# Projection weight loads moved from SyncE to ScalarE, and two weight splits moved by one slot, in a two-layer decoder step

## What is computed

```python
def fox_project(h, w_qkvf, b_f):
    q, k, v, f = jnp.split(h @ w_qkvf, [D_MODEL, 2 * D_MODEL, 3 * D_MODEL], axis=-1)
    logf = jax.nn.log_sigmoid((f + b_f).astype(jnp.float32))
def fox_attend(q, cum_q, q_pos, k, v, cum_kT, k_pos):
    s = jnp.einsum('bqhd,bkhd->bhqk', q, k) * (HEAD_DIM ** -0.5)
    s = s + jnp.transpose(cum_q, (0, 2, 1))[..., None] - cum_kT[:, :, None, :]
    p = jax.nn.softmax(jnp.where(mask, s, NEG_INF), axis=-1)
    return jnp.einsum('bhqk,bkhd->bqhd', p, v)
```

## The kernel before

| step | tile 3i+4 | tile 3i+5 | tile 3i+6 |
|---|---|---|---|
| load, SyncE | slot 0 (from pair 1 on), line 658 | slot 4, line 654 | slot 8, line 656 |
| high half, ScalarE | slot 2, line 1347 | slot 6, line 1377 | slot 12, line 1422 |
| low half, GpSimd | round 3, line 917 | round 7, line 919 | round 14, line 924 |

## Time and profile before

### The profile page before, as it was taken

One profiled execution on the slowest core, in us unless ns is written; L12 is line 12 of the kernel. 1 busy time (PEld: TensorE's weight loads), 2 busy tenths in 40 slices (PEclk: granted clock), 3 DMA queues, 4 the chain that ended last, 5 costly groups with the idle time before them and its releaser, 6 DMA issues.

```text
span 2634.0 us, 45278 instructions
## 1 busy us (share of the span) xinstructions
PE 2559.6 (97%) x18462; PEld 2344.4 (89%) x18462; DVE 1657.1 (63%) x1948; ACT 966.3 (37%) x1838; POOL 1532.8 (58%) x870
## 2 busy tenths in 40 slices
PE   7899999999899999999999999999999999999999
PEld 5677666666589999999999999999989999999998
DVE  5677666676556566666666663444466666666665
ACT  4466766667745322222222241111432222222223
POOL 2867566686237866666666652222586666666661
PEclk9999999999999999999999999999999999999999
DMA  8777777877731111111211111111111121111112
GB/s 292 248 254 250 265 267 272 294 251 257 260 105 50 57 49 49 49 49 53 61 49 49 57 33 49 48 45 32 53 49 49 51 61 51 49 49 49 49 57 82
DMA packets 240573, 292.33 MB, mean 111 GB/s; under 512 B 12995, under 2 KB 193316, under 8 KB 240246
## 3 DMA queue, kind: packets, MB, share of 16 engines
q1 hardware_dynamic: 216658, 271.40, 31.8%
q10 hardware_dynamic: 23572, 17.12, 2.0%
q0 software_dynamic: 144, 1.05, 0.1%
HBM read 268.28 MB, written 21.28 MB: 110 GB/s over the span
## 4 chain that ended last, share of the span: by engine, by line
PE 78%; POOL 8%; DVE 5%; issue 3%; ACT 2%; DMA 2%; SPq 0%; DVEq 0%; POOLq 0%; ACTq 0%
PE PS L2079 32%; PE PS L1634 10%; PE PS L2171 6%; PE PS L2172 6%; PE PS L2170 6%; PE PS L2007 6%; POOL kpage L867 4%; PE PS L1850 2%; DMA kpage<-in_cache_k 2%; PE PS L1852 2%; PE PS L1851 2%; PE PS L1790 1%; DVE pt L2428 1%; DVE s_raw L2365 1%; PE PS L2043 1%
## 5 line engine op out<-in xcount | busy, mean ns | idle before, releaser
L840 POOL TENSOR_TENSOR w_lo<-raw,w_hi 128x1024 fp32r<-128x1024 f32 (+2 forms) x98 | 245.1, 2501 | 641.2 <-ACT w_hi L1539 282.8
L2079 PE MATMUL PS<-a_all,wb 128*128 128x258 f32 x3488 | 571.5, 284 | 5.2 <-POOL wb L1000 3.6
L2079 PEld LDWEIGHTS PS<-a_all,wb 128*128 128x128 f32 x3488 | 486.5, 190 | 6.1 <-POOL wb L1000 4.0
L2687 DVE TENSOR_TENSOR x_res<-PS,x_res 128x1032 f32<-128x1032 f32 (+2 forms) x400 | 399.5, 1015 | 75.0 <-PE PS L2172 65.2
L867 POOL TENSOR_TENSOR kpage<-kpage,q_bc 128x1024 f32<-128x1024 f32 x128 | 307.3, 2416 | 102.1 <-DMA kpage<-in_cache_k 79.2
L2079 PE MATMUL PS<-c_lo,wb 128*128 128x258 f32 x1744 | 352.5, 284 | 0.0
L2171 PE MATMUL PS<-wb,w_hi 128*128 128x344 f32 x960 | 308.0, 321 | 0.0
L2172 PE MATMUL PS<-wb,w_lo 128*128 128x344 f32 x960 | 307.8, 321 | 0.0
L2170 PE MATMUL PS<-wb,w_hi 128*128 128x344 f32 x960 | 305.7, 318 | 0.0
L2079 PEld LDWEIGHTS PS<-c_lo,wb 128*128 128x128 f32 x1744 | 271.8, 190 | 0.0
L1634 PE MATMUL PS<-a_all,w_hi 128*128 128x344 f32 x1152 | 213.4, 321 | 0.4 <-ACT rinv L1129 0.4
(11 more groups left out here) (351 smaller groups left out, 5467.1 us busy)
## 6 DMA issues: line engine op xcount, KB each, us to landing
kpage<-in_cache_k SPq DMA_DIRECT2D x128, 512.0 KB, 4.7
vpage<-in_cache_v SPq DMA_DIRECT2D x128, 512.0 KB, 5.3
raw<-in_w_ffn_in SPq DMA_DIRECT2D x88, 512.0 KB, 4.2
raw<-in_w_ffn_out SPq DMA_DIRECT2D x44, 512.0 KB, 3.6
raw<-in_attn_w_qkvf SPq DMA_DIRECT2D x24, 512.0 KB, 6.1
vpage<-in_attn_w_qkvf SPq DMA_DIRECT2D x24, 512.0 KB, 6.1
raw<-in_conv_w_in SPq DMA_DIRECT2D x24, 512.0 KB, 3.7
out<-raw ACTq DMA_DIRECT2D x16, 512.0 KB, 7.0
```

The source lines that it names most:

```text
L840: gp.tensor_tensor(w_lo[s][:, 0:kts, 0:cols], raw[s][:, 0:kts, 0:cols], w_hi[s][:, 0:kts, 0:cols].bitcast(F32), ALU.subtract).then_inc(w_l ...
L2079: ins = pe.matmul(out[:, b, :], w[:, k, :], h[:, k, x, b * (HN // 2):(b + 1) * (HN // 2)], start=k == 0 and n == 0, stop=k == HK - 1 and n ...
L2687: ins = dve.tensor_tensor(x[:, at:at + n, :], src, x[:, at:at + n, :], ALU.add)
```

## The change

The three `load_q` calls go from SyncE's pair loop to ScalarE's, where a function of the same name issues the same transfers with the same wait. They come after `key_rows` in slot 0, after `total` in slot 5 and after the exponentials of slot 10. On ScalarE the high half of tile 3i+4 goes from slot 2 to slot 3, behind the exponentials, and that of tile 3i+5 from slot 6 to the end of slot 7. On GpSimd the low half of tile 3i+5 goes from round 7 to round 8; the other two low halves and the high half of tile 3i+6 stay where they are. The five loads issued ahead of the pair loop stay on SyncE.

```diff
@@ SyncE, pair(i) @@
             for n in range(NSLOT):
-                    if n == 4 and i < LAST:
-                        load_q(3 * i + 5)
-                    if n == 8 and i < LAST - 1:
-                        load_q(3 * i + 6)
-                    if n == 0 and 0 < i < LAST:
-                        load_q(3 * i + 4)
@@ GpSimd, pair(i) @@
                     if n == 3 and i < LAST:
                         low_q(3 * i + 4)
-                    if n == 7 and i < LAST:
+                    if n == 8 and i < LAST:
                         low_q(3 * i + 5)
@@ ScalarE @@
+            def load_q(n):
+
+                act.wait_ge(w_lod[w_slot(n - 1)], w_count(n - 1))
+                act.dma_start(raw[0][:, :, :], w_tile(w_qkvf, 0, KT, n % 3 * D + n // 3 * P)).then_inc(w_raw[0], 16)
@@ ScalarE, pair(i) @@
                 key_rows(i)
+                if 0 < i < LAST:
+                    load_q(3 * i + 4)
                 sample(0)
...
                 normalise(i, 7)
-                if more:
-                    high_q(3 * i + 4)
                 sample(2)
 
                 exponentials(i, 3)
                 if not more:
                     high_values(i)
+                if more:
+                    high_q(3 * i + 4)
                 total(i, 6)
...
                 total(i, 5)
+                if more:
+                    load_q(3 * i + 5)
                 sample(5)
...
                 sample(6)
-                if more:
-                    high_q(3 * i + 5)
-                else:
+                if not more:
                     early_tile(0)
 
                 exponentials(i, 7)
                 high_turned(i, 2)
                 total(i, 4)
+                if more:
+                    high_q(3 * i + 5)
                 sample(7)
...
                 exponentials(i, 10)
+                if i < LAST - 1:
+                    load_q(3 * i + 6)
                 store_output(i, 3)
```

## The result

The kernel after takes 2645.5 us (median of 6 runs, 2643.2 to 2646.9), the kernel before 2634.1 us (median of 6, 2631.9 to 2637.2). The ratio is 1.004, with an interval of 1.003 to 1.005: **11.4 us slower**. The forecast was 2636 us in a range from 2622 to 2648; the time lies in the range and outside the 0.2% that the text counted as no change. It is closest to rival 1, 2643 us. The forecast's own change, +3.2 us, was 8.2 us short.

The account below looks back on a forecast made before the run. TensorE's matmuls were taken to bound the pair loop, with 20.6 us open. Terms -3.5 + 8.7 - 4 + 2 = +3.2 us on the 2632.4 us median gave 2636 us, range 2622 to 2648.

Parts of the forecast that it names:

- rival 1: Slower: GpSimd's lateness at the key split is paid in full, gains of the later value split are lost; 2643 us, chance 0.25.
- Part A: Weight loads leave SyncE's page queue for ScalarE's: 19 of 24 move, no page was held back by them; 0 us.
- Part B: Value weights' high split goes from slot 6 to 7 on ScalarE, so slot 7's exponentials start earlier; -3.5 us.
- The first paragraph: Pair loop's first seven pairs: TensorE's matmuls cover 555.3 of 575.9 us, so at most 20.6 us can be won.
- Part C: Key weights' low split on GpSimd in slot 3 starts later, so pages behind it reach VectorE late; +8.7 us.
- Part D: Value weights' low split on GpSimd goes behind slot 8's pages, ending VectorE's waits for them; -4 us.
- Part E: Same load bytes at other times, slots 5 and 10, beside key pages whose landings may lengthen; +2 us.
- Rival 3: Slower: slot 5's load lands too late for slot 7's split, stopping ScalarE in all seven pairs; 2649 us, chance 0.05.
- Rival 2: Faster: the late key split is caught up, the value split's gains come in full; 2619 to 2623 us, chance 0.25.

## Why the prediction was right and wrong

- **Part A, 0 us: right.** The two runs that differ in the issuing queue lie 0.9 us apart, inside their intervals. By the Trainium skill's DMA: Bandwidth & Descriptors, section Issuing engines are not separate DMA queues, a new issuer could save the issues' time; these runs agree that it gives no more, and show not even that.
- **Part B, -3.5 us: wrong, it is about 0.** The step that failed is the subtraction "without the split the exponentials could start 0.95 us earlier". They did. But the step went from there straight to the end time, without asking whether TensorE waited for them. In slots 7 and 8 of the kernel before it stood still in two pairs: 0.96 us in pair 4, for another piece of ScalarE's work, and 0.51 us in pair 5, for these exponentials:

```profile
549.57 0.50 PE L1790 MATMUL PS<-k_hi,q_hi 64*128 64x512 f32 x2 [0.51 <-ACT probs L1192]
```

Slot 7 of pair 5 takes 4.7 us in all six kernels with the split in slot 7, and 5.3 us in the other eight. But slot 8 of that pair takes 5.8 to 6.1 us in the six and 5.4 in the others: what one slot won the next gave back. The first paragraph had the number to ask with, 20.6 us open, and never cut it by slot: 8.3 us are in slots 0 and 1, 8.6 in slots 11 to 14, 3.7 in slots 7 to 10, and none in slots 2 to 6. The Trainium skill, Perfetto Trace Analysis, section Identifying the Most-Contended Engine, judges TensorE's headroom by its weight loads; these filled 7.00 of the 8.69 us of slots 7 and 8 in pair 2, and none of the 1.69 us that they left was had. For what a move can win here, the matmul rows were the nearer guide.
- **Part C, +8.7 us: right in place and mechanism, 7.1 to 8.0 us in size.** Pair 0 paid 2.7 of 3.6, pair 5 1.5 of 1.5, pair 6 3.2 of 3.1, pair 1 and pairs 2 to 4 nothing.
- **Part D, -4 us: mis-sized, 0.8 us and not told from 0.** The step that failed is the same: waits of VectorE were added up as time won. Those in the earlier trace rows did vanish, and pair 2's slots 9 and 10 are 1.9 us shorter (in the kernel after all of it is spent again in slots 11 to 14 of that pair). Of the like waits in pairs 3 to 6 nothing came back to speak of: TensorE had next to no open time there. The 1.9 us show a limit of that measure, too. The same stretch before and after, and in it the products with the values in slots 9 and 10, first before, then after:

```profile
306.53:318.72 12.19, 11.01 (x77) 7.57 (x76) 10.99 (x20) 9.55 (x26) 9.52 (x5) 1.00 0.47 153
310.67:320.98 10.31, 9.67 (x75) 7.41 (x74) 10.25 (x19) 9.36 (x26) 8.18 (x5) 1.00 0.57 175
...
309.58 1.90 PE L1826 MATMUL PS<-pt,v_pack 128*128 128x256 f32 x8
314.83 1.83 PE L1826 MATMUL PS<-pt,v_pack 128*128 128x256 f32 x8
...
313.56 1.22 PE L1831 MATMUL PS<-pt,v_pack 128*128 128x256 f32 x8
317.82 1.12 PE L1831 MATMUL PS<-pt,v_pack 128*128 128x256 f32 x8
```

Open time fell by 0.5 us only, and busy time by 1.3, at a granted clock of 1.00 in both: the same eight products took 0.7 us less in each slot. A row of several matmuls holds short stops that count as busy. So the 20.6 us are not the most that can be won, as the first paragraph had it.
- **Part E, +2 us: mis-sized, 5 us.** "At slot 10 one is put beside pages and one taken from beside the pages of slot 8: even" is the step that failed. TensorE's open time in slots 7 to 10 is 3.7 us in all seven pairs, so a page that is late there was mostly hidden; in slots 11 to 14 it already stands open for 8.6 us, mostly behind late pages, and a load beside those pages lengthens that. The sign that the text named, page landings still near 4.7 us, came true all the same: a median does not show single late pages. Its bound of 8 us held.
- **The sum.** 0 + 0 + 7.2 - 0.8 + 5 = 11.4 us, with 7.2 between the price by ratio and that by medians. That it meets the measured 11.4 so well is luck, since each term is known to a microsecond at best. Against the forecast's +3.2, B lacks 3.5 us, D 3.2 and E 3, and C was 1.5 too high. The range held the time only because it had been stretched past rival 1. The chances had given 0.40 to a balance of gains in slots 6 to 8 against C, and 0.25 to rival 1, in which C is paid and B and D give nothing. Rival 1 is what happened, with E larger.
- **Rival 3** was 0.05 and costed for all pairs; it came in one pair of one run, where a load took 13.0 us. Its margin in the kernel after was small: the slowest of the 19 loads took 12.6 us there.
- **Rival 2** needed C to be caught up by projection steps; TensorE ran dry in slot 6 of pairs 0 and 5, or just ahead of it in pairs 0 and 6, all the same.

## What to carry to other kernels

Before a wait on a helper engine is priced, cut the open time of the bounding engine by stage: an earlier start was worth little where that engine had none, and a later start was still paid where the cover was thin. Compare the lengths of the stages as well, since short stops can hide in rows that count as busy. A transfer is best put beside work that has room for it: here its place relative to the pages that are already waited for was worth some 5 us, and who issues it nothing that could be told. Removing the largest wait from a list only shows the next one, if the late thing is what stands ahead of both.

## What was not expected of the hardware

TensorE's granted clock made part of the loss. In pair 4 of the kernel after, the windows view around the wait of 2.61 us:

```profile
497.50:500.10 2.60, 0.00 (x0) 0.00 (x0) 1.99 (x4) 0.99 (x1) 2.60 (x2) 0.69 0.75 237
500.10:505.80 5.70, 5.70 (x24) 4.94 (x28) 3.73 (x5) 1.19 (x2) 5.70 (x4) 0.54 0.91 328
505.80:511.00 5.20, 5.20 (x47) 3.58 (x45) 2.52 (x3) 1.85 (x4) 5.20 (x3) 1.00 0.79 275
```

and around the wait of 2.14 us at the same place before, and a later stretch of it behind a wait of 1.80 us in pair 6:

```profile
492.00:494.80 2.80, 0.66 (x3) 0.19 (x1) 1.99 (x4) 2.73 (x6) 2.80 (x2) 1.00 0.93 360
494.80:498.70 3.90, 3.81 (x24) 2.87 (x28) 3.47 (x5) 1.09 (x2) 3.90 (x3) 1.00 0.79 269
661.00:664.00 3.00, 3.00 (x23) 1.26 (x21) 2.41 (x3) 1.20 (x2) 3.00 (x3) 0.50 0.59 232
```

The same 24 matmuls (values, turned probabilities, two projection steps, the first four of a value page) take 5.7 us mostly at the lower level, 1.2 GHz, and 3.9 us at 2.4 GHz. So behind a wait that was 0.5 us longer the same work took 1.8 us more. In the kernel after TensorE had also stood still for 0.61 us at 495.38, 1.5 us ahead of that wait. The length of the wait alone does not tell: 2.14 us left the clock at 1.00 in pair 4 before, 1.80 us did not in pair 6.

The second surprise is the spread of equal transfers: projection loads of 512 KB landed in 3.8 to 8.0 us in the earlier trace rows, and in up to 12.6 and 13.0 us where one left beside value pages, a query row and a store.
